# One constant of the layout: the last of sixteen activation tiles at the same pitch as the others (LAST = 60 to LAST = 0)

## What is computed

```
h = rms_norm(x) ; proj = h @ w_in                      # first block
x = x + concat(rwkv7_mixer(proj), gdn_mixer(proj)) @ w_out
h = rms_norm(x) ; x = x + (silu(h @ w_gate) * (h @ w_up)) @ w_down
x = rms_norm(x)
a = rms_norm_2(x)                                      # second block
x = x + fox_mixer(a)                                   # a @ w_in, attention of 16 heads, @ w_out
x = x + conv_ffn(rms_norm_2(x))                        # 3-tap convolution, silu gate, @ w_down
```

## Time and profile before

| | us |
|---|---|
| three executions | 2507.58, 2510.59, 2513.11 |
| their median | 2510.59 |
| span of the profiled execution (first to last instruction) | 2505.9 |
| TensorE busy | 2439.3 (97%) |
| VectorE busy | 1484.8 (59%) |
| ScalarE busy | 1122.4 (45%) |

### The profile page before, as it was taken

One profiled execution on the slowest core, in us unless ns is written; L12 is line 12 of the kernel. 1 busy time (PEld: TensorE's weight loads), 2 busy tenths in 40 slices (PEclk: granted clock), 3 DMA queues, 4 the chain that ended last, 5 costly groups with the idle time before them and its releaser, 6 DMA issues.

```text
span 2505.9 us, 57361 instructions
## 1 busy us (share of the span) xinstructions
PE 2439.3 (97%) x24650; PEld 2411.0 (96%) x24650; DVE 1484.8 (59%) x1683; ACT 1122.4 (45%) x1061; POOL 114.1 (5%) x93
## 2 busy tenths in 40 slices
PE   7999978989999999999999999999999999999998
PEld 7999968889999999999999999989999999999998
DVE  6557597665555555554444567674576666665444
ACT  4334424354444444443344443454455555544332
POOL 3000050000200000000020200000200000000000
PEclk9999989999999999999999999999999999999999
DMA  7455400116555555556665565625555555555554
GB/s 232 166 187 196 135 6 4 37 69 193 188 190 197 188 195 190 193 192 192 194 192 194 169 237 200 218 86 191 187 194 191 194 189 196 187 197 188 200 187 148
DMA packets 171387, 431.72 MB, mean 172 GB/s; under 512 B 17614, under 2 KB 23387, under 8 KB 170107
## 3 DMA queue, kind: packets, MB, share of 16 engines
q1 hardware_dynamic: 170027, 422.30, 50.0%
q10 hardware_dynamic: 1232, 7.52, 0.8%
HBM read 427.59 MB, written 2.17 MB: 171 GB/s over the span
## 4 chain that ended last, share of the span: by engine, by line
PE 91%; DVE 7%; ACT 2%; issue 1%; DMA 0%; DVEq 0%; SPq 0%; ACTq 0%
PE ps L1947 28%; PE ps L1948 28%; PE ps L1949 28%; DVE LOW L1073 1%; ACT HIW L606 1%; PE ps L2101 1%; DVE TM L1346 0%; ACT H_ROWS L648 0%; DVE LO L1350 0%; DVE TT L1347 0%; DVE CV L1380 0%; DVE GT L1362 0%; PE ps L2139 0%; DVE TMP L1293 0%; PE ps L2045 0%
## 5 line engine op out<-in xcount | busy, mean ns | idle before, releaser
L1073 DVE TENSOR_TENSOR LOW<-RAW,HIW 128x2048 fp32r<-128x2048 f32 (+1 forms) x397 | 911.9, 2297 | 921.9 <-ACT HIW L606 921.8
L1947 PE MATMUL ps<-H_ROWS,HIW 128*128 128x256 f32 x4928 | 1367.3, 277 | 20.1 <-DVE LOW L1073 17.5
L1948 PE MATMUL ps<-H_ROWS,HIW 128*128 128x256 f32 x4928 | 1366.1, 277 | 0.0
L1949 PE MATMUL ps<-H_ROWS,LOW 128*128 128x256 f32 x4928 | 1364.9, 277 | 0.0
L606 ACT ACTIVATE HIW<-RAW 128x2048 fp32r<-128x2048 f32 (+1 forms) x397 | 760.8, 1917 | 1196.4 <-PE ps L1949 1192.5
L1947 PEld LDWEIGHTS ps<-H_ROWS,HIW 128*128 128x128 f32 x4928 | 928.4, 188 | 22.1 <-DVE LOW L1073 18.5
L1949 PEld LDWEIGHTS ps<-H_ROWS,LOW 128*128 128x128 f32 x4928 | 928.9, 188 | 0.0
L1948 PEld LDWEIGHTS ps<-H_ROWS,HIW 128*128 128x128 f32 x4928 | 928.1, 188 | 0.1
L1947 PE MATMUL ps<-HID,HIW 128*128 (+1 forms) x1408 | 388.7, 276 | 0.0
L1948 PE MATMUL ps<-HID,HIW 128*128 (+1 forms) x1408 | 388.6, 276 | 0.0
L1949 PE MATMUL ps<-HID,LOW 128*128 (+1 forms) x1408 | 388.6, 276 | 0.0
(11 more groups left out here) (365 smaller groups left out, 1515.3 us busy)
## 6 DMA issues: line engine op xcount, KB each, us to landing
RAW<-in_ffn_w_up SPq DMA_DIRECT2D x264, 512.0 KB, 4.3
RAW<-in_ffn_w_down SPq DMA_DIRECT2D x176, 512.0 KB, 4.5
RAW<-in_fox_w_in SPq DMA_DIRECT2D x98, 512.0 KB, 4.4
RAW<-in_w_in SPq DMA_DIRECT2D x96, 512.0 KB, 4.1
RAW<-in_ffn_w_gate SPq DMA_DIRECT2D x88, 512.0 KB, 3.7
RAW<-in_w_out SPq DMA_DIRECT2D x32, 512.0 KB, 5.0
RAW<-in_fox_w_out SPq DMA_DIRECT2D x32, 512.0 KB, 4.8
INV<-rows_out ACTq DMA_DIRECT2D x4, 1024.0 KB, 7.5
```

The costliest lines, as they stand in the source:

```text
L1073: V.tensor_tensor(LOW[:, u_const % 4, 0:n], RAW[:, u_const % 4, 0:n], HIW[:, u_const % 2, 0:n].bitcast(F32), ALU.subtract).then_inc(lo_mad ...
L1947: mm(o_, hi_w, h_hi, start=start, stop=False)
L1948: mm(o_, hi_w, h_lo, start=False, stop=False)
L1949: i = mm(o_, lo_w, h_hi, start=False, stop=stop)
```

## The change

The constant LAST becomes 0, so tile 15 of each row of H_ROWS follows tile 14 directly, as every other tile follows its neighbour. Everything that writes or reads tile 15 goes through H, so writers and readers move together. The kernel before and the kernel after have the same instructions in the same order on all five engines, and the same waits; only addresses differ.

```diff
 TP = 260
 PAD = TP - T
-LAST = 60
+LAST = 0
 T_WA, T_G0, T_G1 = 0, 1, 2
```

## The result

| | before | after |
|---|---|---|
| executions | 20 | 20 |
| median, us | 2511.03 | 2532.69 |
| lowest and highest, us | 2507.58, 2520.3 | 2501.57, 2562.89 |
| span of the profiled execution, us | 2505.9 | 2529.2 |

The kernel after is slower: 1.0053 times the time of before, 95% interval 1.003 to 1.0075. That ratio leaves out the executions that lie over 1.5% above the fastest of their kernel (three of after); by the medians of all executions it is 1.0086. The more telling number is the spread. Before, twenty executions lie within 13 us; after, six of them are at 2502 to 2517 us, twelve at 2526 to 2543 and two at 2547 and 2563.

The account below looks back on a forecast made before the run. TensorE's matmul stream was taken to bound the kernel. 38 groups at 0.15 us, with other terms near nothing, sum to 5.8 us off: median from 2510.6 to 2504.8 us, range 2501.0 to 2509.0.

Parts of the forecast that it names:

- What bounds the kernel: Whole kernel: TensorE, busy 2439.3 of 2505.9 us, sets the time; what its matmul stream saves is saved at the end.
- The address as the cause of tile 15's cost: Groups of 384 matmuls: tile 15 takes 119.2 ns a matmul because it starts 48 bytes past a multiple of 64.
- The cover of the banks and of VectorE's low weights: Steady groups: low weights ready 0.70 us early, first bank 0.9 us; no wait replaces the 0.15 us gain.
- the value put in for the changed tile and its neighbours: Every group: 113.3 ns a matmul, 43.52 us instead of 43.67, saving 0.15 us in each of 38 groups.
- The bounds: Gain from tile 15's matmuls: at least nothing if the address isn't the cause, at most about 5.8 us.
- The rival on the slow side, the clock: Phase heads: more half-clock stretches, about 1.5 us each; seven more would give 2515.3 us; chance 0.02.
- The other rivals: Tile 15: address not the cause, 2510.6 us, chance 0.08; or half the gain, 2508 us, chance 0.06.
- The scatter: Executions of before: 5.5 us apart (2507.58 to 2513.11), so a median may be off by 2 or 3 us.

Follow-up runs that it names:

- the low row alone: Kernel before, with LAST = 60 kept only for low parts and the high part of tile 15 at the common pitch: median 2572.56 us, ratio 1.0229 to before.
- the thirteen splits: Kernel after (LAST = 0) with 13 matmuls, behind places where TensorE waited, each split into two of 128 columns: median 2505.53 us, 0.9971 of before.
- the kernel with four shifted tiles: Against LAST = 0: low-row tiles 4 to 7 moved 240 bytes, 8 to 14 256, 15 496; high-row tile 15 240: median 2542.9 us.

## Why the prediction was wrong

**What bounds the kernel** was right: the time follows TensorE's stream, 23.9 us more of it busy, 23.3 us more span.

**The address as the cause of tile 15's cost** was right. Its matmuls went from 119.2 to 113.3 ns, in all groups that ran at the fast pace, and the group period from 43.67 to 43.52 us. The cover of the banks and of VectorE's low weights held; no new wait came. The lowest execution is 6.0 us below the lowest of before, with 5.8 forecast.

**The step that failed is the value put in for the changed tile and its neighbours**, 113.3 ns for all 384 matmuls of a group, and so 43.52 us, in every group. I took 113.3 ns for a property of an aligned tile. It is one of two paces at which aligned tiles run, and the kernel before had a tile every 43.67 us that turns the stream to it. I priced the unaligned tile at what it cost and at nothing for what it did. Without it a slow pace taken behind a wait lasted to the end of its phase, 27 us in the one long phase of after that the trace shows slow, instead of the rest of one group, at most 1.7 us.

**The bounds** ran from no gain to 5.8 us; I left a loss out, since only addresses move. The rival on the slow side, the clock, was the wrong mechanism: the granted clock is 1.00 throughout the slow stretch. It also holds a slip: seven such stretches make 2515.3 us, 0.19% above 2510.6 and not over 0.2%. The other rivals didn't happen either.

**The scatter** of before I took as given, an uncertainty of 2 or 3 us on a median. At least a part of it had a cause in the trace. The first gate-up groups of the two feed-forwards, alike in every instruction, took 45.5 and 46.1 us in the trace of before, and the 0.6 us between them were the slow stretch shown above. I averaged the pace over one good group and compared tiles within it, but never the same group between phases. Nor did I ask why the deviating address should have been worth its visible price: not that it was there, but that all fifteen other tiles were so exactly alike for 700 us at a time, while the start of the kernel was not.

**What stays open.** It is shown that the stream has two paces, that a stop can leave either, that aligned matmuls keep it, and which of five patterns turn it which way. What in TensorE or the memory makes them is not: the slow pace comes with 4 ns more on one weight load in three, on any of the three lines, and no run took that apart. Whether the chip shifts how often the slow pace is taken is open as well. Why 240 bytes turn it surely and 48 bytes only sometimes, and why the low row alone turns it to slow, is open too. The short stop in the second down projection has no cause in the views that I read. It falls 288 matmuls into the phase, where TensorE's loop over four units returns for the first time; the first down projection has the same loop and no stop. The expectation for the thirteen splits says that every trace has it, which is wrong: the two that come to this place at the slow pace, of the kernel after and of the low row alone, show none.

## What to carry to other kernels

A steady stream can have more than one steady state; before a deviation in it is taken out for its visible price, compare the stream's pace between phases and executions, not only beside the deviation. Take the scatter of a kernel's executions as something to be explained: here a difference of 7.4 us between two executions held the two paces. And a run of eight executions that all fall well proves little when an execution can take one of several states and nothing says what sets the odds: LAST = 64 looked 0.4% faster in one run, and was no better than LAST = 0 in the next.

## What the runs showed of the hardware

- A stream of triples of 128 x 128 by 256 matmuls with aligned operands runs at 113.3 or 117.8 ns a matmul at the same granted clock of 1.00, and keeps the one it has for up to 710 us. At the slow one a weight load in three takes 192 ns and not 188.
- A moving operand 240 bytes past a multiple of 256 costs 5.9 ns a matmul (119.2 ns) when both parts are so placed, and 2.5 ns when the low part alone is (115.8 ns, 11.12 us for the 96 matmuls of tiles 4 to 7 in the kernel with four shifted tiles, the first ones behind the change included; 115.5 ns further on). The Trainium skill, "SBUF — State Buffer", Specifications (TRN2), with its 16-byte lines doesn't tell these addresses from the aligned ones; the trace does.
- Splitting one matmul of 256 columns into two of 128 costs 0.125 us, and turned the pace to fast each of the ten times that the stream was slow before it.
